# The output projection of an encoder layer as eight 2x2 cells of seven block products

## What is computed

```python
z = rmsnorm(x, g_attn) @ w_in
...
x = x + jnp.concatenate([o_a, o_m, o_b], axis=-1) @ w_out
up = rmsnorm(x, g_ffn) @ w_up
up, f_conv_new = causal_dwconv(up, f_conv_past, conv_f_w, conv_f_b)
val, gt = jnp.split(up, 2, axis=-1)
x = x + (jax.nn.gelu(gt) * val) @ w_down
```

## Time and profile before

| | |
|---|---|
| median of 3 runs | 2307.22 us (2307.16 to 2307.92) |
| the profiled execution, time | 2306.84 us |
| its span | 2305.0 us |
| PE busy | 2296.9 us (100%) |
| DVE busy | 1780.4 us (77%) |
| ACT busy | 1157.4 us (50%) |
| POOL busy | 307.6 us (13%) |

### The profile page before, as it was taken

How to read it: one execution, slowest core, us unless ns; L and a number is a source line. 1 busy time by engine, 2 the same in 40 slices (tenths; PEclk the granted TensorE clock), 3 DMA queues, 4 the chain that set the end, 5 groups by cost and what they waited for, 6 DMA issues and landing times.

```text
span 2305.0 us, 44976 instructions
## 1 busy us (share of the span) xinstructions
PE 2296.9 (100%) x18000; PEld 2278.5 (99%) x18000; DVE 1780.4 (77%) x2410; ACT 1157.4 (50%) x1885; POOL 307.6 (13%) x258
## 2 busy tenths in 40 slices
PE   9999999999999999999999999999999999999999
PEld 8999999999999999999999999999999999999999
DVE  6788667665424888888888888888888988787876
ACT  4566454454322555555555555545555555454543
POOL 5100000000122111121121111111211110000000
PEclk9999999999999999999999999999999999999999
DMA  9532333332533434344343344343434678676864
GB/s 297 148 83 80 108 91 92 103 89 83 183 102 109 121 104 135 118 126 128 118 136 118 118 130 124 113 140 110 141 115 146 174 197 209 157 207 161 215 146 102
DMA packets 479286, 309.89 MB, mean 134 GB/s; under 512 B 10856, under 2 KB 457320, under 8 KB 479096
## 3 DMA queue, kind: packets, MB, share of 16 engines
q1 hardware_dynamic: 470664, 289.97, 42.6%
q0 software_dynamic: 8432, 17.27, 4.5%
HBM read 255.79 MB, written 53.51 MB: 134 GB/s over the span
## 4 chain that ended last, share of the span: by engine, by line
PE 95%; DVE 3%; issue 1%; ACT 0%; DMA 0%; SPq 0%; DVEq 0%; ACTq 0%
PE out L2706 21%; PE out L2707 21%; PE out L2708 21%; PE out L2339 9%; PE out L2342 9%; PE out L2340 9%; PE out L2350 2%; PE out L2452 1%; DVE ring_l L2013 1%; DVE fl L2247 0%; PE out L2545 0%; PE out L2434 0%; ACT ring_h L1421 0%; DMA pair<-in_w_up 0%; DVE t L2006 0%
## 5 line engine op out<-in xcount | busy, mean ns | idle before, releaser
L2013 DVE TENSOR_TENSOR ring_l<-pair,ring_h 128x1024 fp32r<-128x1024 f32 (+1 forms) x384 | 455.2, 1185 | 177.2 <-ACT ring_h L1421 177.0
L1421 ACT CAST ring_h<-pair 128x1024 fp32r<-128x1024 f32 (+1 forms) x384 | 383.1, 998 | 321.3 <-DVE pair L2040 228.4
L2706 PE MATMUL out<-t,ring_h 128*128 128x272 f32 x1536 | 442.3, 288 | 1.2 <-DVE ring_l L2013 0.7
L2708 PE MATMUL out<-t,ring_l 128*128 128x272 f32 x1536 | 441.4, 287 | 0.0
L2707 PE MATMUL out<-t,ring_h 128*128 128x272 f32 x1536 | 441.0, 287 | 0.0
L2339 PE MATMUL out<-xh,wh 128*128 128x272 f32 x1600 | 439.4, 294 | 0.0
L2340 PE MATMUL out<-xl,wh 128*128 128x272 f32 x1600 | 429.8, 287 | 0.0
L2706 PE MATMUL out<-fh,ring_h 128*128 128x272 f32 x1344 | 388.2, 289 | 2.6 <-DVE ring_l L2013 1.7
L2707 PE MATMUL out<-fl,ring_h 128*128 128x272 f32 x1344 | 387.0, 288 | 0.0
L2708 PE MATMUL out<-fh,ring_l 128*128 128x272 f32 x1344 | 385.2, 287 | 0.0
L2706 PE MATMUL out<-b,ring_h 128*128 128x272 f32 x1152 | 332.2, 288 | 0.0
(11 more groups left out here) (287 smaller groups left out, 3962.8 us busy)
## 6 DMA issues: line engine op xcount, KB each, us to landing
pair<-in_w_up SPq DMA_DIRECT2D x192, 512.0 KB, 4.0
raw<-in_w_in SPq DMA_DIRECT2D x36, 1024.0 KB, 5.6
pair<-in_w_down SPq DMA_DIRECT2D x64, 384.0 KB, 4.8
pair_d<-in_w_down SPq DMA_DIRECT2D x64, 384.0 KB, 4.8
h_forms<-fb SPq DMA_DIRECT2D x24, 816.0 KB, 6.2
fr<-h_forms SPq DMA_DIRECT2D x24, 816.0 KB, 7.5
out_yT<-stage POOLq DMA_DIRECT2D x31, 544.0 KB, 7.9
raw<-in_w_out SPq DMA_DIRECT2D x16, 1024.0 KB, 5.9
```

The lines of the kernel that those rows point to most:

```text
L1421: nc.scalar.copy(ring_h[:, n % 3, 0:width(i)], weight_of(p, i)).then_inc(op_hi, 1)
L2013: v.tensor_tensor(ring_l[:, n % 3, 0:w], weight_of(p, i), ring_h[:, n % 3, 0:w].bitcast(F32), ALU.subtract).then_inc(op_lo, 1)
L2706: mm(out, w_high, high[:, k, :], start=opens and k == 0, stop=False, skip_group_check=True)
L2708: ins = mm(out, w_low, high[:, k, :], start=False, stop=k == tiles - 1, skip_group_check=True)
```

## The change

The output projection's 16 units become eight cells (`O_CELLS`) of seven block products, in the same form as the feed-forward cells; `multiply_o` issues them. The mix's forms take the place of `xh` and `xl`: B11, B21, B22 are split whole, and T1 to T4 are made in place in `rows` by four GpSimd instructions and a small VectorE one, then split whole. Since `rows` holds the forms, x is loaded again into it when they are split (`load_x_again`), and each product is added onto it from its accumulator bank (`add_o`, L2238); cell 0's results wait in `kept_a` to `kept_c` and in banks until then. The weight quarters of the projection come through `pair0` alone (with `s1_buf` for the fourth quarter of odd cells), S3 is made by GpSimd. The forms of x1 for the feed-forward part are made and split at the end, during the last projection cell and the first feed-forward cell (FFN cell 0), half of the steps on GpSimd.

```diff
+O_CELLS = KT // 2
+O_OPS = PROD * O_CELLS
+O_FIRST = (1, 5, 2, 6, 3, 7, 4)
+O_ORDER = (1, 5, 6, 2, 7, 3, 4)
...
-ORDER_FIRST = (1, 2, 5, 6, 7, 4, 3)
+ORDER_FIRST = (1, 5, 6, 2, 7, 4, 3)
...  (GpSimd)
+            nc.gpsimd.tensor_tensor(b12, b12, b11, ALU.subtract).then_inc(mix_t, 1)
...
+            make_s2_first()
+            make_o_s3(0)
...
+            nc.gpsimd.tensor_tensor(right(0, n), right(K8, KT - 1), right(0, n), ALU.subtract).then_inc(mix_t, 1)
...
+            nc.gpsimd.tensor_tensor(b11, b12, b11, ALU.subtract).then_inc(mix_t, 1)
+            pool.wait_ge(xlo, KT + 4)
+            nc.gpsimd.tensor_tensor(b21, b21, b12, ALU.subtract).then_inc(mix_t, 1)
...
+            for d in range(1, O_CELLS):
+                if d < O_CELLS - 1:
+                    make_o_s3(d)
+                if d == 5:
+                    pool.wait_ge(x1_scaled, K8)
+                    nc.gpsimd.tensor_tensor(b12, b12, b11, ALU.subtract).then_inc(x1_t, 1)
+                square_x1(2 * d - 2)
+                if d == O_CELLS - 1:
+                    make_o_s3(d)
+                square_x1(2 * d - 1)
+
+            e = EARLY
+            pool.wait_ge(x1_hi, 1)
+            nc.gpsimd.tensor_tensor(bl[0][:], b11, bh[0][:].bitcast(F32), ALU.subtract).then_inc(x1_lo_pool, 1)
+            pool.wait_ge(x1_lo, 1)
+            pool.wait_ge(x1_scaled, K8 + e)
+            nc.gpsimd.tensor_tensor(right(0, e), right(K8, K8 + e), right(0, e), ALU.subtract).then_inc(x1_t, 1)
...  (VectorE, cell 0)
+            lo_mix(3, t1l[:], right(0, K8), t1h[:])
+            lo_o(2, 0)
+            read_g(3)
+            make_o_s4(0)
+            mix_g(3)
...  (TensorE)
-            for m in range(KT - 2):
-                unit(U_OUT + m, first=KT if m == 0 else None)
...
-            last_units()
+            def multiply_o(p, d):
+
+                n = o_at(p, d)
+                if d == 0:
+                    pe.wait_ge(xlo, KT + {1: 1, 5: 3, 2: 4, 6: 5, 3: 6, 7: 7, 4: 8}[p])
...
+                pe.wait_ge(op_lo, n + 1)
...
+                block(out, n % 3, *forms[p], K8, opens).then_inc(product, 1)
+
+            for d in range(O_CELLS):
+                for p in O_ORDER if d else O_FIRST:
+                    multiply_o(p, d)
```

More of the change, by code:

```diff
@@ L514, in x_tiles, with left, right, o_quarter @@
             return range(at[u], at[u + 1])
-        def form_of(k):
-            return k // K8, k % K8
+        def left(first, end):
+            return rows[:, first:end, 0:HALF]
+        def right(first, end):
+            return rows[:, first:end, HALF:ROWS]
+        def o_quarter(d, q):
+            return s1_buf[:, :] if q == 3 and d % 2 else quarter[0][:, q, :]
+        def o_weight(p, d):
+            return o_quarter(d, {1: 0, 5: 2, 6: 0, 2: 1, 7: 2, 3: 1, 4: 3}[p])
+        def o_added_after(p, d):
+            return PROD * (d - 1) + O_ORDER.index(p) + 1
+        def o_loaded(engine, d, q):
+            if q < 3:
+                engine.wait_ge(quarter_in[0][q], 16 * (d + 1))
+            else:
+                engine.wait_ge(odd_a22_in if d % 2 else quarter_in[0][3], 16 * (d // 2 + 1))
         def quarter_of(g, q):
@@ new lines, in _, with to_first, add_o @@
+            lo_mix(8, t4l[:], left(K8, KT), t4h[:])
+            make_o_s1(1)
+            lo_o(1, 1)
+            make_o_s2(1)
+            lo_o(5, 1)
+            def to_first(k, c, src):
+                dst = rows[:, k, c * HALF:(c + 1) * HALF]
+                v.tensor_tensor(dst, src, dst, ALU.add).then_inc(o_first, 1)
+            def add_o(p, d):
+                dve.wait_ge(product, o_at(p, d) + 1)
+                if p == 1:
+                    dve.wait_ge(x_in[d % 4], 16 * (d // 4 + 2))
+                if p in (2, 7, 3):
+                    dve.wait_ge(o_added, o_added_after({2: 1, 7: 5, 3: 6}[p], d))
+                bank = {2: y_bank, 5: q_bank, 3: q_bank}.get(p, x_bank)(d)
+                k = 2 * d + (p in (5, 7, 4))
+                c = HALF * (p in (5, 6, 7, 3))
+                dst = rows[:, k, c:c + HALF]
+                v.tensor_tensor(dst, bank, dst, ALU.add).then_inc(o_added, 1)
@@ L2669, in _, with block @@
-            last_units()
-            pe.wait_ge(flip_read, flips_before(HM + HA))
+            forms = {1: (bh[0], bl[0]), 2: (bh[1], bl[1]), 3: (bh[2], bl[2]),
+                     5: (t1h, t1l), 6: (t2h, t2l), 7: (t3h, t3l), 4: (t4h, t4l)}
+            def block(out, slot, high, low, tiles, opens):
+                for k in range(tiles):
+                    w_high, w_low = (t[:, slot, k * P:(k + 1) * P] for t in (ring_h, ring_l))
+                    mm(out, w_high, high[:, k, :], start=opens and k == 0, stop=False, skip_group_check=True)
+                    mm(out, w_high, low[:, k, :], start=False, stop=False, skip_group_check=True)
+                    ins = mm(out, w_low, high[:, k, :], start=False, stop=k == tiles - 1, skip_group_check=True)
+                return ins
```

721 lines of the change are left out of this document (433 added, 288 removed).

## The result

The changed kernel takes 2330.51 us (median of 4 runs, 2329.93 to 2331.41) against 2307.36 us (4 runs, 2307.16 to 2307.92): 23.2 us slower, ratio of the runs 1.0100 with a 95% interval of 1.0087 to 1.0113. The forecast was 2338 us. The time lies 7.5 us under it, within the range, and on the side that was given 0.82.

The account below looks back on a forecast made before the run. TensorE was taken to bound the kernel. Span: 2305.0 - 24.0 - 1.8 + 0.5 + 20.6 + 4.9 + 31.2 = 2336.4 us, so a median of 2338 us, with a range from 2308 to 2356.

Parts of the forecast that it names:

- the side that was given 0.82: Whole kernel: the change makes it slower, chance 0.82, against 0.15 for faster and 0.03 for the same.
- The matmuls: Output projection: 1536 matmuls become 1344; the 192 that go, at 0.1252 us each, save 24.0 us.
- the first rival: Added work: GpSimd's long instructions let VectorE through, so few waits and 2288 us, faster; chance 0.13.
- The port: VectorE instructions with two SBUF inputs and GpSimd tensor_tensors exclude each other, whole instruction by whole instruction; adds from banks go free.
- GpSimd's price: GpSimd forms: 2.17 ns a number plus 0.19 us fixed, so 4.91 us for 2176 numbers.
- Start and cell 0: First projection cell: starts 0.5 us late, seventh product near 626, waits of 20.6 us in the cell.
- the sum on the port: Cell 0 before its seventh product: GpSimd's 23.9 us plus VectorE's 28.9 make 52.8, so at least 20.2 us lost.
- the walk: Engines' written orders followed with forecast durations: waits of 20.6 us in cell 0, 4.9 in cells 1 to 6, 31.2 after.
- Cells 1 to 6: Middle projection cells: 4.9 us lost, 1.8 in cell 2 and 3.1 in cell 5; bounds nothing and 14.5.
- Cell 7 and FFN cell 0: Port carries 67.6 us against 39.1 of TensorE: at least 28.5 lost; forecast 12.9 and 18.3, together 31.2.
- The FFN cell that goes: Old first feed-forward cell: its 1.8 us of lost TensorE time go, as its work is arranged anew.
- The clock: Rival: long waits drop TensorE to 1.2 GHz, 3 to 5 us each, 2347 to 2353 us; chance 0.15 (no fall 0.65).

Follow-up runs that it names:

- The last experiment: Changed kernel with every two-input GpSimd instruction from the mix's first form to x1's last cut to one column per tile, arithmetic left out: 2284.48 us.
- the memsets: Changed kernel with GpSimd's T1 to T4 in cell 0 replaced by memsets of the same rows, nearly as long but without input: 2316.81 us.
- the run with 25 such steps: Changed kernel with 20, 20 and 48 unused small matmuls ahead of the products of T1, B21 and T2 in cell 0: 2331.83 us.

## Why the prediction was right, step by step

- *The matmuls.* The step of 0.1252 us holds, 24.0 us go. The last experiment comes near to the first rival's world, with GpSimd's work not beside VectorE's but gone: 2284.5 us, where the prediction gave that rival 2288.
- *The port.* The mechanism, that two-input instructions of the two engines exclude each other, is right: the rows above and the memsets show it. In cell 0 it carries all but some 2 of 15.6 us; over all cells GpSimd's two-input instructions are worth 46 us, their own lateness included. By the Trainium skill ("SBUF — State Buffer", "Who interferes with whom") the contention needs a GpSimd instruction that reads SBUF; the memsets, which read nothing, agree: 0.73 us instead of 4.99.
- *GpSimd's price.* 4.91 us were read off a line through smaller sizes; T1 took 4.92.
- *Start and cell 0.* The seventh product was to start near 626. TensorE's timeline, where a wait ends or that product begins:

```profile
588.80 0.39 PE L2889 MATMUL out<-b,ring_h 128*128 128x272 f32 x1
...
595.37 0.39 PE L2889 MATMUL out<-t,ring_h 128*128 128x272 f32 x1 [3.31 <-DVE t L2190]
...
603.29 0.59 PE L2889 MATMUL out<-b,ring_h 128*128 128x272 f32 x1 [3.11 <-DVE b L2190]
...
616.17 0.57 PE L2889 MATMUL out<-t,ring_h 128*128 128x272 f32 x1 [7.07 <-DVE ring_l L2164]
616.53 0.43 PE L2890 MATMUL out<-t,ring_h 128*128 128x272 f32 x1
616.76 0.43 PE L2891 MATMUL out<-t,ring_l 128*128 128x272 f32 x1
...
626.86 0.34 PE L2889 MATMUL out<-t,ring_h 128*128 128x272 f32 x1
```

It starts at 626.86. The low part of T4, the last item of the sum on the port, ends just before, at 624.32 + 2.42 = 626.74:

```profile
624.32 2.42 DVE L2190 TENSOR_TENSOR t<-rows,t 128x2176 fp32r<-128x2176 f32 x1 [0.23 <-ACT t L1518]
```

The sum had 52.8 us from 573.06 on; GpSimd's first form starts at 573.90, and from there it took 52.8. The cell loses 20.1 us (41.1 less 21.0), 20.6 were predicted; the start is 1.15 us late instead of 0.5. The waits are shorter than the walk had them (3.3, 3.1 and 7.1 for 3.8, 5.2 and 10.3), and most of the rest is slow steps, which the sum had left out: from 616.53 on two starts lie 0.23 us apart. So the loss of the cell is right by its cause, and its split into waits is not.
- *Cells 1 to 6.* A mis-sized term: 2.65 us are lost, not 4.9. Cell 2 loses 0.5 instead of 1.8, cell 5 2.0 instead of 3.1.
- *Cell 7 and FFN cell 0.* 12.0 and 15.9 us, for 12.9 and 18.3. The last is the largest error, 2.4 us. The bare sum of the port had 28.5 us for the two and called it a lower bound; 27.9 were lost. The 2.7 us that the walk put on top did not come. T2 and the gate pieces meet GpSimd in another order than in the walk; which pair saves the time was not tried.
- *The FFN cell that goes.* The window of the earlier trace rows ended before the cell did. Timed to the start of its successor (803.89), it lost 2.6 us and not 1.8.
- *The sum.* 2305.0 - 24.0 - 2.6 + 1.15 + 20.1 + 2.65 + 12.0 + 15.9 = 2330.2; the rest of the kernel behind these cells is 1.1 us shorter (1500.0 for 1501.1), for which I have no cause (it is 1499.1 to 1501.4 us in the profiles of the other runs): 2329.1 against a span of 2328.7. But for the start, every error goes the same way, so the forecast is too high by nearly their sum.
- *The clock.* The forecast rested on the branch without a fall of the clock; the fall had a chance of 0.15, with 3 to 5 us for each long wait. It came, already behind waits of 3.1 and 3.3 us: the clock granted from 603.3 to 606.3 us is 0.50, and 24 steps of 0.227 us instead of 0.125 make a product 2.4 us longer. In the three cells the slow steps add 12.9 us. By the rule of the Trainium skill ("TensorE: Matmul & The Clock Gate", "What's actually happening") an idle TensorE falls to 1.2 GHz, and the trace agrees. The branch was wrong, then, and its price too: a slow product for the most part runs out in the next wait for VectorE, and with 5.3 us of the slow steps taken away in the late cells the median fell by 1.0 us, with half of them gone in cell 0 it rose by 1.3. What the fall costs is what stands behind a cell's last wait: in cell 0 the run with 25 such steps needs 1.1 us more than the one with 14. That the time still came out by the branch without a fall is luck.

## What to carry to other kernels

Before you give GpSimd work "because it is idle", add its two-input instructions to VectorE's instructions with both inputs in SBUF as if they were one engine, with GpSimd at 2.1 times the price, and compare that sum with TensorE's time for the stretch. Here the sum was 52.8 against 32.6 us in cell 0 (20.1 lost) and 67.6 against 39.1 in the last two cells (27.9 lost). It is near a floor and not always the loss: with the mix's forms on VectorE the sum of cell 0 is 52.8 - 19.1 + 9.0 = 42.7 us, which would lose 10.1, and the cell lost 14.0. If the sum is larger than TensorE's time, the work belongs on VectorE, on ScalarE where one input is enough, or into an earlier stretch. A TensorE clock that falls behind a wait is a symptom while another engine's lag sets the next wait; behind the last wait of a stretch its slow steps count. Test it with filler matmuls before you treat it, and look whether they fill the wait: 48 were too few for a wait of 7 us.

## What the runs showed that I had not expected

The exclusion holds for the smallest instructions too, when it is GpSimd that has to wait. Timeline of GpSimd in the kernel with everything cut:

```profile
573.42 0.22 POOL L1050 TENSOR_TENSOR rows<-rows 128x8 f32<-128x8 f32 x1 [72.32 <-ACT rows L1302]
578.69 0.53 POOL L1050 TENSOR_TENSOR pair<-pair 128x1 f32<-128x1 f32 x1 [5.06 <-DVE ring_l L2172]
580.58 2.24 POOL L1050 TENSOR_TENSOR pair<-pair 128x1 f32<-128x1 f32 x1 [1.36 <-DVE ring_l L2172]
```

VectorE's row beside the last of them:

```profile
580.35 4.47 DVE L2198 TENSOR_TENSOR b<-rows,b 128x2176 fp32r<-128x2176 f32 x2
```

One number a partition takes 0.53 or 2.24 us, where eight took 0.22 with no two-input instruction of VectorE beside them. At 580.58 VectorE had just begun a low part of 2176 numbers (580.35), which is done at 580.35 + 2.33 = 582.68; GpSimd's instruction ends at 582.82. GpSimd's memsets, in turn, run through: each pair of 2176 numbers takes 3.90 us, 0.9 ns a number, both beside VectorE's rows at 574.03 and beside those at 598.20.
